# Scoring cached keys in sixteen small array tiles: keys turned by VectorE instead of TensorE

## The chip, the cores and the metric

The kernel runs on one core of one Trainium2 chip, in one launch. All arithmetic is in 32-bit floats. The metric is the device time in microseconds (us) from the first to the last instruction of the program; lower is better. Work on the core goes to TensorE (PE, matrix products out of SBUF into the eight PSUM banks), VectorE (DVE), ScalarE (ACT), GpSimd (POOL, here mostly an issuer of DMAs) and SyncE (SP, which only issues DMAs). Each engine runs its own instructions in order, and they meet through counting semaphores.

## What is computed

One decoder step: layer 0 has latent attention (MLA), layer 1 sliding-window attention, and each layer ends in a mixture of experts. Prompt tokens (512) and 8 sampled sequences of 4 new tokens go through it together. The change touches one thing alone, the attention of the sampled tokens over their cached past in layer 0:

```python
past = cache_pool[page_table].reshape(b, past_len, MLA_ROW)      # 8 x 4096 rows of 256 + 64
c_past, kr_past = past[..., :KV_LORA], past[..., KV_LORA:]
q_lat = jnp.einsum('bthd,chd->bthc', q_nope, w_uk)
s_past = (jnp.einsum('bthc,bkc->bhtk', q_lat, c_past).astype(jnp.float32)
          + jnp.einsum('bthr,bkr->bhtk', q_rope, kr_past).astype(jnp.float32)) * MLA_SCALE
...
p = jax.nn.softmax(jnp.concatenate([s_past, s_new], axis=-1), axis=-1).astype(c.dtype)
o_lat = (jnp.einsum('bhtk,bkc->bthc', p[..., :past_len], c_past)
         + jnp.einsum('bhtk,bkc->bthc', p[..., past_len:], c))
o = jnp.einsum('bthc,chd->bthd', o_lat, w_uv).reshape(b, t, MLA_HEADS * V_HEAD)
```

Each sequence has 32 query rows (8 heads, 4 tokens) and 4096 cached rows of 320 numbers, which lie in 32 pages of 128 rows, scattered in HBM and found through a page table.

## The kernel before

Everything is placed by hand: SBUF regions, PSUM banks, the order on each engine and every semaphore wait. The part around the change, which this text calls the cached stage, comes after the prompt's attention in layer 0 and before its output projection.

**Pages.** A page is loaded with its 128 rows on the 128 partitions, 320 floats each, 160 KB a page. Two SBUF buffers of 32 pages take turns (`pages[b % 2]`). Those of sequences 0 and 1 are loaded early by POOL. For b from 2 on, a buffer comes free in quarters of 8 pages as the value product of b - 2 passes over it: `page_mm` counts three of them, `pv_mm` the last. SP loads the first and third quarter, POOL the second and fourth. What this text calls quarter 1 of b is the first eight pages, semaphore `pages0` or `pages1`.

**Keys.** The value product wants cached rows on partitions, as they are loaded. The scores want the 320 features on partitions, so each page is transposed. For a quarter of a sequence (eight pages), `keys_T(b, t)` on PE makes 20 transposes of 128x128 (`flip`, L2021) into banks 2 to 6, ACT copies three banks and DVE two (L752, L1324) into `kT`, two buffers in turn, and `scores(b, t)` makes 12 products of 32 query columns by 256 keys over 128 or 64 features, in four column groups of the array (L2016), into banks 0 and 1.

**Softmax.** DVE takes the largest score of the first half, then of the second (`largest_so_far`, `largest`, L1329 and L1336), ACT makes the exponentials in two halves (`weigh`, L923 and L926), PE transposes the weights (`weights_T`), ACT and DVE copy them, and `values(b)` makes 33 products against the untransposed pages into bank 7.

**Order.** In PE's order one sequence is interleaved with the next: `keys_T(b, 0)`, `scores(b - 1, 3)`, `keys_T(b, 1)`, `scores(b, 0)`, `weights_T(b - 1)`, `values(b - 1)`, `keys_T(b, 2)`, `scores(b, 1)`, `keys_T(b, 3)`, `scores(b, 2)`.

**Ahead and behind.** Ahead of the loop the weight block `w_uk` is transposed (16 flips), the queries are multiplied by it (`qlat_mm`, 32 records), copied (L752, L1309, L1313), and the scores over the new tokens are made (`new_mm`). Behind the loop come the output projection, whose weights SP loads once `values(6)` is done (`mla_wo`), the router, and the experts, whose weights stream from HBM.

A 32-bit product appears in the trace as two pairs of LDWEIGHTS and MATMUL, a transpose as one; such a pair is called a record here. A line of a helper stands for all its callers: L2016 is every product, L2021 every transpose, L752 every copy by ACT.

Of the kernel before, what the change touches and what calls it, by code (L numbers as in the profile page):

```python
# [24 lines left out]
PAGES = 32  # L25
PHYS = 320
# [52 lines left out]
        tp_mm2 tp_mm3 tp_mm4 tp_mm5 tp_mm6""",  # L79
# [48 lines left out]


def keys_at(b, t):  # L130

    return 4 * b + t + max(0, b - (t < 2))


def weights_at(b):

    return 4 * (b + 1) + 2 + b if b < NB - 1 else 4 * NB + b
# [41 lines left out]
def build(nc, a, o):  # L179
    with ExitStack() as ctx:  # L180
# [118 lines left out]
        odd_pair = pair_buffers()  # L299
        qsw = m.take(TOK)  # L300
        even_pair = pair_buffers()
        qr, qn, kn, v_m = zip(even_pair, odd_pair)
        cqjunk = p_m[0][:, 0:QL]

        s = Arena(mem, pair_from - 2 * TOK, WORDS)
        kT_both = [s.take(5 * 4 * P) for _ in range(2)]
        kT = [q.rearrange("p (n g c) -> p n g c", n=5, g=2) for q in kT_both]
        wukT = kT_both[1][:, 0:H * 2 * P].rearrange("p (h k c) -> p h k c", h=H, k=2)
        p_s = s.take(8 * P)
        pT_s = cqT.rearrange("p k t -> p (k t)")[:, 0:8 * P].rearrange("p (n c) -> p n c", n=8)  # L310
        o_s = s.take(NB, CL)
        qlat = cqT.rearrange("p k t -> p (k t)")[:, 8 * P:8 * P + 2 * NB * NS].rearrange("p (k b q) -> p k b q", k=2, b=NB)
        qmix, qodd1, qodd2 = (s.take(NB, NS) for _ in range(3))
        sel32 = s.take(NS)
        over = Arena(mem, cq_at, cq_at + 2 * QL + CL + 2 * DR + QL)
        olatT = over.take(2, H, NS)
        smask = over.take(NB, NS)
# [3 lines left out]
        pTn = s.take(NS)  # L321
        mn, m_s, m2_s, nm_s, l_s, l2_s, ln_s, w_s = (s.take(NB) for _ in range(8))
        mg, lg_s, dg = (s.take(4, NB) for _ in range(3))
        mt, lt_s = (s.take(NB) for _ in range(2))
        assert s.at <= WORDS - 2 * 2 * H * DN and qsw.shape[1] == TOK
        wkvb = Arena(mem, WORDS - 2 * 2 * H * DN, WORDS).take(2, 2 * H * DN)
# [99 lines left out]
        def _(sp):  # L426
# [57 lines left out]
            for j in range(1, PAIRS):  # L484
                load_pair(j)
            sp.wait_ge(sig["qr_ready"], happened("qr_ready", PAIRS))
            sp.wait_ge(sig["o_mm"], happened("o_mm", UNITS - 2 * PT))
            sp.dma_start(wkvb, wkv).then_inc(sig["wkvb_in"], DMA)
# [115 lines left out]
        def _(g):  # L604
# [42 lines left out]
            def experts(L):  # L647
# [11 lines left out]
                g.wait_ge(sig["h_ready"], happened("h_ready", NORMED[2 * L + 1]))  # L659
                g.dma_start(gain, row(a["norm_ffn"][L])).then_inc(sig["gain_in"], DMA)  # L660
# [87 lines left out]
        def _(act):  # L748
# [160 lines left out]
            act.drain().then_inc(sig["wuk_act"], 1)  # L909

            def keys_T(b, t):

                at = keys_at(b, t)
                act.wait_ge(sig["qk_mm"], happened("qk_mm", 4 * b + t - 1))
                for bank, n in ((2, 0), (4, 1), (6, 2)):
# [1923 lines left out]
```

## Time and profile before

| | us |
|---|---|
| median of 3 runs | 1846.52 (1845.17 to 1849.54) |
| the profiled execution, its span | 1842.6 |
| TensorE busy | 1743.9 (95%) |
| VectorE busy | 602.8 (33%) |
| ScalarE busy | 381.9 (21%) |
| a period of the cached stage, from one value product's start to the next | 21.3 |

The page gives no time of the profiled execution apart from its span. The span is cut into 40 slices of 46 us; the cached stage fills slices 5 to 8. The granted clock of TensorE is given as a share of 2.4 GHz, so 0.50 is 1.2 GHz.

### The profile page before, as it was taken

What the parts mean: (1) busy time and instruction counts of PE and PEld (TensorE: products, weight loads), DVE (VectorE), ACT (ScalarE), POOL (GpSimd) and SP (SyncE); (2) the same over time, 40 slices, a digit from 0 to 9 for tenths busy, and PEclk for the clock granted to TensorE, in tenths of its full rate; (3) what the DMA queues carried; (4) which work ended last, traced back from release to release, by engine and by line L of the source; (5) the groups of instructions that cost most, each with busy time, mean ns of one, the idle gap of its engine ahead of it and who ended that gap; (6) DMA issues with size and microseconds to landing.
All of it is one profiled execution on the core that took longest, in us unless ns stands there. A gap on an engine that the chain in (4) does not pass through costs nothing.

```text
span 1842.6 us, 29042 instructions
## 1 busy us (share of the span) xinstructions
PE 1743.9 (95%) x9946; PEld 871.1 (47%) x9947; DVE 602.8 (33%) x1586; ACT 381.9 (21%) x858; POOL 214.1 (12%) x312
## 2 busy tenths in 40 slices
PE   7899899999899999999999899999899999999995
PEld 5466676655544444434344445455444444333342
DVE  2334343331522222222222556764322222212223
ACT  2233344431111111111011224342011111111112
POOL 1231014410001000000010201000000010000010
PEclk9899999999989999999999999999899999999998
DMA  6252137775449999999998800032899999999974
GB/s 181 68 155 88 50 116 237 254 253 208 159 182 404 414 421 417 412 419 419 415 418 350 303 14 1 20 138 85 347 375 412 422 414 418 414 421 408 418 307 151
DMA packets 80624, 511.63 MB, mean 278 GB/s; under 512 B 20917, under 2 KB 39302, under 8 KB 54074
## 3 DMA queue, kind: packets, MB, share of 16 engines
q1 hardware_dynamic: 61962, 461.35, 62.1%
q0 software_dynamic: 18576, 49.16, 8.1%
q8 instruction: 51, 0.84, 0.2%
q14 instruction: 35, 0.29, 0.1%
HBM read 498.07 MB, written 26.52 MB: 285 GB/s over the span
## 4 chain that ended last, share of the span: by engine, by line
PE 75%; DMA 14%; DVE 5%; issue 2%; ACT 2%; DVEq 1%; SPq 0%; POOL 0%; ACTq 0%; POOLq 0%
PE ps L2016 65%; DMA mem<-in_moe_w_up 11%; PE ps L2021 10%; ACT mem L752 1%; DMA mem<-in_x_sample 1%; DMA mem<-in_c_masks 1%; DVE mem L1794 0%; DMA mem<-moe_rows_back 0%; DMA mem<-in_cache_mla 0%; DMA moe_rows_back<-mem 0%; DVE mem L1765 0%; DMA mem<-in_swa_sinks 0%; DVE mem L1336 0%; ACT mem L923 0%; ACT mem L926 0%
## 5 line engine op out<-in xcount | busy, mean ns | idle before, releaser
L2016 PE MATMUL ps<-mem 128*64 128x512 f32 (+14 forms) x7970 | 1510.1, 485 | 62.2 <-DMA mem<-moe_rows_back 14.0
L2016 PEld LDWEIGHTS ps<-mem 128*64 128x64 f32 (+4 forms) x7970 | 641.9, 145 | 837.8 <-issue 747.6
L752 ACT ACTIVATE mem<-ps 128x512 f32<-128x512 f32 (+4 forms) x370 | 205.7, 567 | 621.9 <-PE ps L2016 425.2
L2021 PE MATMUL ps<-mem 128*128 128x128 f32 (+1 forms) x1976 | 274.8, 280 | 28.9 <-DMA mem<-in_x_prompt 6.9
L2021 PEld LDWEIGHTS ps<-mem 128*128 128x128 f32 (+1 forms) x1976 | 234.2, 171 | 125.0 <-issue 101.7
L1636 DVE TENSOR_TENSOR mem<-mem,ps 64x512 f32<-64x512 f32 x64 | 44.2, 690 | 433.2 <-ACT mem L995 433.2
L692 POOL DMA_INDIRECT moe_rows_back<-mem x64 | 57.3, 896 | 853.5 <-DVE mem L1653 842.6
L995 ACT ACTIVATE mem<-ps 64x512 f32<-64x512 f32 x64 | 37.7, 589 | 557.8 <-PE ps L2016 557.8
L1653 DVE COPY mem<-ps 64x512 f32<-64x512 f32 x64 | 44.4, 693 | 147.2 <-PE ps L2016 147.2
L1324 DVE COPY mem<-ps 128x512 f32<-128x512 f32 x64 | 44.2, 692 | 77.0 <-PE ps L2021 73.0
L644 POOL DMA_DIRECT2D mem<-in_cache_mla x96 | 51.7, 538 | 104.2 <-PE ps L2016 94.2
L1617 DVE COPY mem<-ps 64x512 f32<-64x512 f32 x32 | 22.2, 694 | 89.4 <-PE ps L2016 89.4
L624 POOL DMA_DIRECT2D mem<-in_cache_mla x64 | 34.4, 538 | 114.1 <-issue 114.1
L1062 ACT ACTIVATE mem<-mem 128x256 f32<-128x256 f32 (+1 forms) x64 | 30.3, 474 | 61.6 <-DVEq L1799 61.6
L682 POOL DMA_INDIRECT mem<-moe_rows_in,mem x34 | 33.2, 977 | 79.3 <-issue 79.3
L1794 DVE CUSTOM_DVE_ANT_0 mem<-ps,mem 128x256 f32<-128x256 f32 (+1 forms) x64 | 26.3, 448 | 27.2 <-PE ps L2016 25.1
L1561 DVE TENSOR_TENSOR mem<-mem 128x320 f32<-128x320 f32 x70 | 34.0, 486 | 2.1
L665 POOL DMA_DIRECT2D moe_rows_in<-mem x10 | 5.4, 538 | 237.8 <-DVE mem L1452 237.8
L1720 DVE SCALAR_TENSOR_TENSOR mem<-mem 128x1024 f32<-128x1024 f32 (+1 forms) x16 | 23.1, 1441 | 23.1 <-DMA mem<-moe_rows_back 21.8
L1644 DVE COPY mem<-ps 128x256 f32<-128x256 f32 x64 | 27.2, 425 | 8.1
L867 ACT ACTIVATE mem<-mem 128x128 f32<-128x128 f32 (+3 forms) x32 | 18.0, 561 | 37.8 <-DVEq L1273 37.8
L1622 DVE TENSOR_TENSOR mem<-ps,mem 128x512 f32<-128x512 f32 x32 | 22.1, 692 | 9.8 <-PE ps L2021 9.7
(237 smaller groups left out, 485.2 us busy)
## 6 DMA issues: line engine op xcount, KB each, us to landing
mem<-in_moe_w_gate SPq DMA_DIRECT2D x64, 2048.0 KB, 21.3
mem<-in_moe_w_up SPq DMA_DIRECT2D x64, 2048.0 KB, 27.8
mem<-in_moe_w_down SPq DMA_DIRECT2D x64, 2048.0 KB, 19.4
mem<-in_cache_mla POOLq DMA_DIRECT2D x160, 160.0 KB, 4.4
mem<-in_cache_mla SPq DMA_DIRECT2D x96, 160.0 KB, 5.5
mem<-moe_rows_back SPq DMA_DIRECT2D x8, 1024.0 KB, 8.7
mem<-in_mla_wo SPq DMA_DIRECT2D x1, 4096.0 KB, 14.1
moe_rows_in<-mem POOLq DMA_DIRECT2D x8, 512.0 KB, 3.0
```

The costliest lines, as they stand in the source:

```text
L624: g.dma_start(pages_flat[par][:, bass.ds(j * ROW, ROW)], a["cache_mla"][0][bass.ds(page, 1)].rearrange("a p c -> p (a c)")).then_inc(sig[f ...
L644: g.dma_start(pages[b % 2][:, j, :], a["cache_mla"][0][bass.ds(at[n], 1)].rearrange("a p c -> p (a c)")).then_inc(sig[f"late_pages{b % 2}" ...
L682: g.indirect_dma_start(out=xe[b][0:BLK, :], out_offset=None, in_=rows_in, in_offset=bass.IndirectOffsetOnAxis(ap=fetch_at[b][0:BLK, 0:1].b ...
L692: g.indirect_dma_start(out=rows_back, out_offset=bass.IndirectOffsetOnAxis(ap=store_at[b][0:BLK, 0:1].bitcast(U32), axis=0), in_=ye[b][0:B ...
L752: return act.activation(out, in_, ACT.Copy)
L995: act.activation(sg[BLK:2 * BLK, :], ps[0:BLK, b, :], ACT.Silu).then_inc(sig["silu_ready"], 1)
L1324: v.tensor_copy(kT[t % 2][:, n], ps[:, bank, :].rearrange("p (g c) -> p g c", g=2)).then_inc(sig[f"tp_ev{bank}"], 1)
L1561: v.tensor_tensor(onehot[b], rankm[:, :, cols(q, 1)].broadcast_to([P, TILES, BLK]), slots.unsqueeze(1).broadcast_to([P, TILES, BLK]), ALU. ...
L1636: v.tensor_tensor(hid[0:BLK, :], sg[BLK:2 * BLK, :], ps[BLK:2 * BLK, b, :], ALU.mult).then_inc(sig["hid_ready"], 1)
L1653: v.tensor_copy(ye[b][0:BLK, FF:D], ps[BLK:2 * BLK, 2 + b, :]).then_inc(sig["y1_ready"], 1)
L2016: return pe.matmul(out, lhsT, rhs, start=start, stop=stop)
L2021: return pe.transpose(out, in_, ident[at:at + n, at:at + n])
```

## The change

Pages are no longer transposed on TensorE. VectorE turns each quarter of a sequence, 128 partitions by 2560 floats, with one instruction that transposes 32x32 blocks in place of the 20 flips and five copies. In a block turned so, features lie on 32 partitions and 32 keys along the row, and the four groups of 32 partitions hold four groups of keys. So the query is copied to all four partition groups (`qrep`, made once by ten products with a selection matrix `pick`), and scores are made in sixteen 32x32 tiles of the array: tile (i, g) multiplies 32 features of one partition group i by 32 query columns into PSUM partitions 32g, for 128 keys, and ten such steps sum the 320 features. The scores of the four partition groups lie in banks 0 to 3. PE's order is now `weights_T(b - 1)`, `values(b - 1)`, `scores(b, 0)`, `scores(b, 1)`, and all softmax copies go to ACT. To make room the buffers are moved, `w_uk` and `w_uv` are loaded apart, and three loads get an added wait: `w_uv` for the last score, the MoE's first `down` weights for `oc_mm`, and POOL's load of `gain`, whose place now holds `p_s`.

```diff
+            def keys_T(b, n):
+
+                if b < 2 and n == 0:
+                    v.wait_ge(sig[f"late_pages{b % 2}"], landed(f"late_pages{b % 2}", PAGES))
+                if b >= 2:
+                    name, before_ = (("pages", 0), ("late_pages", PAGES), ("third_pages", 0), ("fourth_pages", 0))[n]
+                    v.wait_ge(sig[f"{name}{b % 2}"], landed(f"{name}{b % 2}", before_ + QUARTER * (b // 2)))
+                if n % 2 == 0:
+                    v.wait_ge(sig["qk_mm"], happened("qk_mm", max(2 * (b - 1) + n // 2 + 1, 0)))
+                v.transpose(keysT[n // 2][:, n % 2 * QUARTER * ROW:(n % 2 + 1) * QUARTER * ROW],
+                            pages_flat[b % 2][:, n * QUARTER * ROW:(n + 1) * QUARTER * ROW]).then_inc(sig["keysT_ready"], 1)
+
+            def largest(b):
+
+                v.wait_ge(sig["qk_mm"], happened("qk_mm", 2 * b + 2))
+                v.tensor_reduce(m_s[:, b:b + 1], ps[:, 0:4, 0:2 * P], XY, ALU.max)
+                v.drain()
+                v.tensor_scalar(nm_s[:, b:b + 1], m_s[:, b:b + 1], mn[:, b:b + 1], -MLA_SCALE, ALU.max, ALU.mult
+                                ).then_inc(sig["nms_ready"], 1)
...
-            for b in range(NB):
-                if b:
-                    keys_T(b, 0)
-                    largest(b - 1)
-                keys_T(b, 1)
-                if b:
-                    weights_T(b - 1)
-                keys_T(b, 2)
-                keys_T(b, 3)
-                largest_so_far(b)
+            for b in range(1, NB):
+                keys_T(b, 0)
+                largest(b - 1)
+                for n in range(1, 4):
+                    keys_T(b, n)
             largest(NB - 1)
...
+            for j in range(ROW // 32):
+                rows, q = (slice(0, P), qlat[:, j // 4]) if j < 8 else (slice(0, DR), qmix[0:DR])
+                last = mm(ps[:, j // 2, j % 2 * NB * NS:(j % 2 + 1) * NB * NS], pick[rows, j % 4, :], q.rearrange("p b q -> p (b q)"), True, True)
+                if j % 2:
+                    last.then_inc(sig["qrep_mm"], 1)
+
+            def scores(b, half_):
+
+                if half_ == 0:
+                    pe.wait_ge(sig["p_s_ready"], happened("p_s_ready", 2 * b))
+                pe.wait_ge(sig["keysT_ready"], happened("keysT_ready", 4 * b + 2 * half_ + 2))
+                blocks = keysT[half_].rearrange("p (m g c) -> p m g c", m=4, g=4)
+                c0 = half_ * P
+                for j in range(ROW // 32):
+                    for i in range(4):
+                        rows = slice(32 * i, 32 * (i + 1))
+                        for g in range(4):
+                            last = mm(ps[g * NS:(g + 1) * NS, i, c0:c0 + P].rearrange("p (m k) -> p m k", m=4),
+                                      qrep[rows, j, b, :], blocks[rows, :, g, 32 * j:32 * (j + 1)], j == 0, j == ROW // 32 - 1)
                 last.then_inc(sig["qk_mm"], 1)
...
             for b in range(NB):
-                keys_T(b, 0)
-                if b:
-                    scores(b - 1, 3)
-                keys_T(b, 1)
-                scores(b, 0)
                 if b:
                     weights_T(b - 1)
                     values(b - 1)
-                keys_T(b, 2)
+                scores(b, 0)
                 scores(b, 1)
-                keys_T(b, 3)
-                scores(b, 2)
-            scores(NB - 1, 3)
             weights_T(NB - 1)
             values(NB - 1)
```

VectorE before, from the score maximum of one sequence through the next one's (L1324 copies turned keys out of PSUM, L1336 is the maximum, L1345 and L1347 copy turned weights):

```order
L1336 TENSOR_REDUCE mem<-ps 128x1 [waits qk_mm]
L1338 TENSOR_SCALAR mem<-mem 128x1
L1324 COPY mem<-ps 128x512 [waits tp_mm3,qk_mm]
L1324 COPY mem<-ps 128x512 [waits tp_mm5]
L1345 COPY mem<-ps 128x512 [waits pv_mm,tp_mm3]
L1347 COPY mem<-ps 32x32 [waits tp_mm6]
L1324 COPY mem<-ps 128x512 [waits tp_mm3,qk_mm]
L1324 COPY mem<-ps 128x512 [waits tp_mm5]
L1324 COPY mem<-ps 128x512 [waits tp_mm3,qk_mm]
L1324 COPY mem<-ps 128x512 [waits tp_mm5]
L1329 TENSOR_REDUCE mem<-ps 128x1 [waits qk_mm]
```

VectorE in the changed kernel, the same place, from `keys_T(2, 0)` on (L1315 turns a quarter, L1321 is the maximum of sequence 1):

```order
L1315 STREAM_TRANSPOSE mem<-mem 128x2560 [waits qk_mm,pages0]
L1321 TENSOR_REDUCE mem<-ps 128x1 [waits qk_mm]
L1323 TENSOR_SCALAR mem<-mem 128x1
L1315 STREAM_TRANSPOSE mem<-mem 128x2560 [waits late_pages0]
L1315 STREAM_TRANSPOSE mem<-mem 128x2560 [waits qk_mm,w_a_in]
L1315 STREAM_TRANSPOSE mem<-mem 128x2560 [waits consts_in]
L1315 STREAM_TRANSPOSE mem<-mem 128x2560 [waits qk_mm,pages1]
L1321 TENSOR_REDUCE mem<-ps 128x1 [waits qk_mm]
```

The waits for arriving pages (`pages0` and `pages1` are quarter 1; `w_a_in` and `consts_in` are the semaphores that quarters 3 and 4 of an even sequence share) were PE's and are VectorE's now, and the first of them stands ahead of the maximum of the sequence before.

TensorE in the changed kernel, one sequence (L2007 is the product helper, L2012 the transpose helper):

```order
L2012 MATMUL ps<-mem 128x128 [waits pT_s_ready,p_s_ready]
L2012 MATMUL ps<-mem 128x128 x3
L2012 MATMUL ps<-mem 128x128 [waits pT_s_ready,p_s_ready]
L2012 MATMUL ps<-mem 128x128 x3
L2012 MATMUL ps<-mem 32x32 [waits pTn_ready]
L2007 MATMUL ps<-mem 32x256 [waits pT_s_ready,o_s_ready]
L2007 MATMUL ps<-mem 32x256 x15
L2007 MATMUL ps<-mem 32x256 [waits pT_s_ready]
L2007 MATMUL ps<-mem 32x256 x15
L2007 MATMUL ps<-mem 32x256 [waits pTn_ready]
L2007 MATMUL ps<-mem 32x128 [waits keysT_ready,p_s_ready]
L2007 MATMUL ps<-mem 32x128 x159
```

Nothing of the next sequence stands between a sequence's last score and its weights any more, and the scores are 320 products a sequence where there were 48.

## Rows read from the trace of the kernel before

**Rows 1.** The page: busy time by engine, and the chain that ended last.

```profile
PE 1743.9 (95%) x9946; PEld 871.1 (47%) x9947; DVE 602.8 (33%) x1586; ACT 381.9 (21%) x858; POOL 214.1 (12%) x312
PE 75%; DMA 14%; DVE 5%; issue 2%; ACT 2%; DVEq 1%; SPq 0%; POOL 0%; ACTq 0%; POOLq 0%
```

**Rows 2.** Busy time per engine in one period, with clock and DMA.

```profile
core 0: us, PE busy (x) PEld busy (x) DVE busy (x) ACT busy (x) POOL busy (x), PEclk, DMA share, GB/s
275.08:296.40 21.32, 21.00 (x251) 14.42 (x252) 7.97 (x15) 9.69 (x20) 8.61 (x16) 1.00 0.75 248
```

**Rows 3.** Timeline of a period: start, length, engine, line, operation, idle before.

```profile
253.79 4.21 PE L2016 MATMUL ps<-mem 128*32 128x256 f32 x66 [0.28 <-ACT mem L752]
...
261.83 2.40 PE L2021 MATMUL ps<-mem 128*128 128x128 f32 x20
...
264.16 1.64 PE L2016 MATMUL ps<-mem 128*32 128x256 f32 x24
```

**Rows 4.** Weight loads of PE near the first pages' arrival.

```profile
265.73 2.17 PEld L2021 LDWEIGHTS ps<-mem 128*128 128x128 f32 x20 [0.41 <-DMA mem<-in_cache_mla]
```

**Rows 5.** DMA between 253.8 and 275.1, in 40 slices.

```profile
DMA  0010554929999979999999999999999999411000
GB/s 0 0 31 0 120 183 77 327 75 351 387 366 406 224 262 356 373 366 325 358 365 380 392 385 361 351 368 375 368 358 346 339 368 313 167 55 46 5 0 0
```

**Rows 6.** The tail of the cached stage, timeline.

```profile
395.76 0.69 DVE L1336 TENSOR_REDUCE mem<-ps 128x1 f32<-128x512 f32 x1 [2.09 <-PE ps L2016]
396.78 0.69 ACT L923 ACTIVATE mem<-ps,mem 128x512 f32<-128x512 f32 x1 [3.59 <-DVE mem L1338]
397.64 0.66 PE L2021 MATMUL ps<-mem 128*128 128x128 f32 x4 [1.94 <-ACTq L925]
398.81 0.79 PE L2021 MATMUL ps<-mem 128*128 128x128 f32 x5 [0.52 <-ACTq L930]
398.84 0.23 ACT L955 ACTIVATE mem<-mem 32x32 f32<-32x32 f32 x1
399.96 6.48 PE L2016 MATMUL ps<-mem 128*32 128x256 f32 x67 [0.36 <-ACT mem L752]
405.85 0.38 ACT L752 ACTIVATE mem<-ps 128x256 f32<-128x256 f32 x1 [6.03 <-PE ps L2016]
```

**Rows 7.** Granted clock of PE in four stretches.

```profile
222.40:232.70 10.30, 8.04 (x37) 0.50 0.01 2
399.90:403.30 3.40, 3.34 (x32) 0.51 0.00 0
403.40:405.70 2.30, 2.30 (x38) 1.00 0.04 7
1198.66:1199.57 0.91, 0.91 (x60) 1.00 0.79 270
```

**Rows 8.** VectorE's groups by form: total, mean ns.

```profile
L1324 DVE COPY mem<-ps 128x512 f32<-128x512 f32 x64 | 44.2, 692 | 77.0 <-PE ps L2021 73.0
L1720 DVE SCALAR_TENSOR_TENSOR mem<-mem 128x1024 f32<-128x1024 f32 x12 | 15.4, 1285 | 22.3 <-DMA mem<-moe_rows_back 21.8
L1561 DVE TENSOR_TENSOR mem<-mem 128x320 f32<-128x320 f32 x70 | 34.0, 486 | 2.1
L1281 DVE TENSOR_SCALAR mem<-mem 128x512 f32<-128x512 f32 x8 | 3.9, 486 | 0.7
```

**Rows 9.** The stretch ahead of the loop, timeline.

```profile
212.00 0.49 DVE L1281 TENSOR_SCALAR mem<-mem 128x512 f32<-128x512 f32 x1
217.44 0.69 DVE L1305 COPY mem<-ps 128x512 f32<-128x512 f32 x1 [4.95 <-PE ps L2021]
219.15 4.01 PE L2016 MATMUL ps<-mem 128*128 128x32 f32 x32 [0.88 <-DVE mem L1305]
225.42 3.18 PE L2016 MATMUL ps<-mem 128*128 128x32 f32 x12 [2.26 <-DVEq L1315]
232.96 1.57 DVE L1354 TENSOR_TENSOR mem<-ps,mem 32x32 f32<-32x32 f32 x8
```

**Rows 10.** The 128 small products of layer 1's samples, timeline of PE.

```profile
1195.42 4.33 PE L2016 MATMUL ps<-mem 64*128 64x256 f32 x130
```

**Rows 11.** The page: the load of the output weights, us to landing.

```profile
mem<-in_mla_wo SPq DMA_DIRECT2D x1, 4096.0 KB, 14.1
```

More of the change, by code:

```diff
@@ L11 @@
 X = mybir.AxisListType.X
+XY = mybir.AxisListType.XY
 P = 128
@@ L284, in build, with pair_buffers @@
         ptab = m.take(NB * PAGES, dt=I32)
+        samples_from = m.at
+        def pair_buffers():
+            return m.take(SEQ), [m.take(SEQ) for _ in range(2)], [m.take(SEQ) for _ in range(2)], m.take(PT, 2 * DN)
+        qsw = m.take(TOK)
+        even_pair = pair_buffers()
         cosT = m.take(TOK)
         sinT = m.take(TOK)
-        pair_from = m.at
         wqp = m.take(3, 2 * (DN + DR))
@@ L320, in build @@
         pn = over.take(NB, NS)
[L321 to L326, printed above, removed]
         r = Arena(mem, work, moe_end)
@@ L493, in _ @@
             sp.dma_start(wo_m, a["mla_wo"][0].rearrange("(k p) n -> p k n", p=P)).then_inc(sig["wo_in"], DMA)
+            sp.wait_ge(sig["qk_mm"], happened("qk_mm", 2 * NB))
+            for k in range(2):
+                sp.dma_start(wuv[:, k], wkv_heads[:, k, :, 1, :]).then_inc(sig["wkvb_in"], DMA)
             def experts(L):
@@ L905, in _ @@
             act.wait_ge(sig["qlat_mm"], happened("qlat_mm", 1))
-            for dst, at in ((qlat[:, 1], slice(0, P)), (qodd1[DR:P], slice(0, DR)), (qodd2[0:DR], slice(DR, P))):
-                copy(dst.rearrange("p b (h t) -> p b h t", h=H),
-                     ps[at, 5, 0:H * NS].rearrange("p (h b t) -> p b h t", h=H, b=NB))
+            copy(qlat[:, 1].rearrange("p b (h t) -> p b h t", h=H),
+                 ps[:, 5, 0:H * NS].rearrange("p (h b t) -> p b h t", h=H, b=NB))
             act.drain().then_inc(sig["wuk_act"], 1)
[L911 to L915, printed above, removed]
-                    count = 4 * b + t if bank == 4 else at
-                    act.wait_ge(sig[f"tp_mm{bank}"], happened(f"tp_mm{bank}", count + 1))
-                    copy(kT[t % 2][:, n], ps[:, bank, :].rearrange("p (g c) -> p g c", g=2)).then_inc(sig[f"tp_ev{bank}"], 1)
+            for n in range(0, 5, 2):
+                act.wait_ge(sig["qrep_mm"], happened("qrep_mm", n + 1))
+                copy(qrep[:, 2 * n:2 * n + 2], ps[:, n, :].rearrange("p (j b q) -> p j b q", j=2, b=NB)
+                     ).then_inc(sig["qrep_act"], 1)
@@ L941, in values @@
                 copy(o_s[:, b, :], ps[:, 7, 0:CL]).then_inc(sig["o_s_ready"], 1)
-            for b in range(NB):
-                keys_T(b, 0)
-                if b:
-                    weigh(b - 1)
-                keys_T(b, 1)
-                if b:
-                    weights_T(b - 1)
-                    values(b - 1)
-                keys_T(b, 2)
-                keys_T(b, 3)
+            for b in range(NB - 1):
+                weigh(b)
+                weights_T(b)
+                values(b)
             weigh(NB - 1)
@@ L1350, in _ @@
+            v.drain().then_inc(sig["qlat_ready"], 1)
+            keys_T(0, 2)
+            for n in range(1, 5, 2):
+                v.wait_ge(sig["qrep_mm"], happened("qrep_mm", n + 1))
+                v.tensor_copy(qrep[:, 2 * n:2 * n + 2], ps[:, n, :].rearrange("p (j b q) -> p j b q", j=2, b=NB)
+                              ).then_inc(sig["qrep_dve"], 1)
+            keys_T(0, 3)
             v.wait_ge(sig["new_mm"], happened("new_mm", 1))
@@ L1409, in add_out @@
                 if n == NS:
-                    out[1] = kT_both[0][0:n, 0:FF]
+                    out[1] = keysT[0][0:n, 0:FF]
                     v.tensor_copy(out[1], ps[n:2 * n, 2 + 2 * (n_ % 2) + 1, :])
```

194 lines of the change are left out of this document (72 added, 122 removed).

## The prediction

> **What bounds the kernel now.** I read the page's busy times and its chain first, then one period of the cached stage as a window by engine, then its timeline, weight loads and DMA, and last the stretches before and behind it. TensorE is busy 95% of the span and 75% of the chain [rows 1]. In one period of the cached stage, 21.32 us, it works 21.00 us at full clock, while VectorE works 7.97, ScalarE 9.69, and the DMA engines 0.75 of the time [rows 2]. So PE sets this stage, and what is taken from it counts until something else ends last. The timeline tells what can be taken: 20 transposes hold PE 2.33 us from start to start, and the 24 records of a quarter's scores 1.57 us [rows 3]. A period has four of each. I call A the start of a value product (253.79 for sequence 0).
>
> **What goes from PE.** 4 x 2.33 = 9.3 us of transposes and 4 x 1.57 = 6.3 us of scores, 15.6 of the 21.3 us. 5.7 us stay: the value product and the transposes of weights.
>
> **What comes to PE.** 320 products, 640 records of 128 keys a sequence. The old scores ran six rounds of four tiles, 256 keys wide, in 1.57 us [rows 3]: a round of 4 records took 0.26 us and 256 keys alone need 0.11 at 2.4 GHz for each, so the four lay side by side. If all sixteen tiles do so too, a half of a sequence is 20 rounds of 16 records with 128 keys, each half a round of 256 keys, 0.13 us: 2.6 us. The 0.26 has the fill of the array and the hand-over in it once per six rounds, here it is once per twenty, so I take 2.3, and 4.6 a sequence. The bounds: if each of the 640 records costs what the densest stretch of the profile shows, 0.91 / 60 = 15 ns [rows 7], it is 9.7 us; by the 128 small products of layer 1 (4.33 us for 130 records with the wait, about 29 ns each [rows 10]) it is 18.4; and if the four row groups take turns, 4 x 4.6 = 18.4 again. PE has room for much of that: the period below leaves it 8 us idle.
>
> **What comes to VectorE.** A turn of 128 x 2560 floats, four a sequence. No row shows the operation. Two reads and a write of 1024 floats take 1285 ns and of 320 take 486 ns, 1.135 ns a float and 123 ns fixed, so 2560 floats take 3.0 us; the 512 floats of a TENSOR_SCALAR in 486 ns are 0.71 ns each, so 1.9 us; the copy out of PSUM, 692 ns for 512, gives 3.46 us [rows 8]. I take 2.8, nearer the upper row, as a turn leaves no float out; the range is 1.9 to 3.5, and 5.6 if it has to go over the data twice. With 2.8, VectorE works 11.2 + 1.5 us a period for turns and the maximum of 1024 scores, less than the period; it would set the period only from (21.3 - 1.5) / 4 = 4.9 us a turn. What VectorE loses, eight copies, and what ScalarE loses, twelve, was hidden behind PE.
>
> The Trainium skill, "Vector Engine (DVE) Microarchitecture Reference", section 3.8, has the transpose sustain one element per cycle in each lane; no row here shows it. By it a turn would be an estimated 2.7 to 2.8 us, and the sum would not move.
>
> **The new wait.** On VectorE `keys_T(b+2, 0)` stands ahead of the maximum of b+1, and waits for quarter 1 of b+2, which the value product of b frees. Behind it on VectorE stand that maximum and all further turns, and for the maximum wait the weights, and so PE's next value product. Before, quarter 1 of sequence 2 let PE go at 265.73 [rows 4], A + 11.9. DMA is nearly idle up to about A + 1.5, then at about 360 GB/s to about A + 18 [rows 5]; the four quarters are freed within 4.2 us and share that rate, hence the late first one. The period is now a chain:
> - A to the arrival of quarter 1: 11.9;
> - the turn: 2.8;
> - from the maximum to the next value product: the tail of the stage shows it without other work on PE. Start of the maximum to start of the exponentials 396.78 - 395.76 = 1.02, plus 0.53 as the maximum now reads 1024 floats, not 512 (at some 1 ns a float); from the exponentials to the value product 399.96 - 396.78 = 3.18, less 0.23 for a small copy whose place changes: 4.5 [rows 6].
>
> Sum 19.2. PE idles some 8 us of it. What idling does to its clock the tail shows: after idling 1.94, 0.52 and 0.36 us PE ran 32 records at clock 0.51 for 3.4 us (1.2 GHz), then at 1.00, so that the value product took about 5.8 and not 4.2 us [rows 6, 7]. A slow start frees the first quarter up to 1.1 us later. So a period lies between 19.2 and 20.3; I take 19.8, and 19.3 for the first one, whose value product follows work. With arrivals 1 us earlier or later, and the bounds of the turn, it is 18.4 to 21. PE's own work is off the path: the value product 5.8, scores 4.6, done at A + 10.4, before the turn is (A + 14.7). DMA's load is off it too: 5.24 MB a period at 360 GB/s is 14.6 us.
>
> **The head.** VectorE's last unit operation ahead is at 212.0 to 212.5 [rows 9]. Two turns of sequence 0 then take 5.6 us to 218.1, while the copy of the transposed `w_uk` stood at 217.44; so the latent queries start at 219.8 and end, with 4.0 us, at 223.9, 0.7 later. The new wait for `qrep` follows: 20 records of 128 x 256. At half clock, which this stretch had before (0.50 [rows 7]), they take 20 x 0.43 = 8.5 us by twice the streaming of a full one, at full clock 4.3; I take 6.4, since part of it waits for copies. From about 224.5 that is 230.9. The new tokens' products (3.18 us for 12 [rows 9]) take 2.2 as part of their wait falls away, to 233.1; the scores of sequence 0 end at 237.8, PE having waited for nothing else, and its maximum follows `keys_T(1, 0)` at 238.4, which is a turn of pages long there. Plus 4.5: A(0) = 243.0 against 253.79, a gain of 10.8 us. The bounds of qrep give 2 us either way.
>
> **The sum.** A(6) = 243.0 + 19.3 + 5 x 19.8 = 361.3. No page is waited for at the end, so A(6) to A(7) is the value product 5.8, scores at about 5.3 (partly at the lower clock), 4.5 and a small copy of 0.3: 15.9. A(7) = 377.2 against 399.96 [rows 6]: 22.8 us less. Of it the head gives 10.8, six periods, 118.3 for 127.8, give 9.5, and the last one, 15.9 for 18.4, gives 2.5.
>
> What lies behind moves along if nothing is late there. The output weights are loaded once `values(6)` is done, 361.3 + 5.8 = 367.1, and take 14.1 us [rows 11]: 381.2, two us before `values(7)` ends at 383. Thin cover; without it up to 1 us. `w_uv`'s 1 MB lies behind the prompt's output projection, the waits of `down` and `gain` behind loads whose users come tens of us later: nothing; were the cover gone, 1 to 3 us. So the profiled execution, 1842.6, becomes 1819.8. The median of the runs shown is 3.9 above that execution: 1823.7, forecast 1824. Its own range, with periods of 18.4 to 21 (6 x 1.3 either way), the head's 2 and the small products' 15 ns bound (not on the path, +5 in the last period), is 1812 to 1834.
>
> **Rivals.**
> 1. *Small products don't fit side by side (slower).* One mechanism: each of the 640 records of a sequence starts too late after the one before, or row groups take turns, 18.4 us a sequence. Then PE's chain is values 5.8, scores 18.4, maximum to values 4.5, small copy 0.2: a period of 28.9, against 21.3. With A(0) 14 later, at 256.8, and seven periods A(7) is 459, 59 us later: about 1905. It decides from (21.3 - 5.8 - 4.7) / 640 = 17 ns a record. For it: layer 1's 29 ns [rows 10]. Against it: 15 ns over 60 records [rows 7], and the four column tiles that ran together [rows 3]. Chance 0.10.
> 2. *A floor on starts.* As one mechanism here: each pair of records starts no closer to the next pair than layer 1's small ones, 29 ns less their wait, some 25 ns a record: 16 us a sequence, a period of 5.8 + 16 + 4.7 = 26.5, 5.2 more than before seven times and 3 or 4 for the head: about 40 us slower, 1887. 60 records in 0.91 us [rows 7] and 24 in 1.57 speak against it only in part, as a product's two halves may start together. Chance 0.05. The Trainium skill, "TensorE: Matmul & The Clock Gate", section "Wait — 56ns, not 53.3ns?", states such a floor, "Start-to-start never drops below ≈25 ns however small N is"; by it the kernel would be slower, and the row with 15 ns disagrees. The same page, in its part on array tiling, reports sixteen 32-row, 32-column tiles as 10.6 times as quick, with 512 columns each; here they have 128, which no row shows.
> 3. *VectorE becomes the bound.* A turn goes over its data twice, 5.6 us. Four of them and 1.5 for the maximum are 23.9 us a period, 2.6 more than before, six times 15.6; the head's two turns take 5.6 longer and the first one after them 2.8, 8.4 of its gain of 10.8, and the last period is as forecast: 15.6 - 2.4 - 2.5 = 10.7 slower. Chained to the arrival of quarter 1 (11.9 + 5.6 + 4.5 = 22.0) it is less than that, so VectorE's own sum holds, but every quarter that VectorE then turns late frees its buffer and the maximum late by up to another 1.5 us a period: 11 to 20, about 1862. For it: nothing shown; against it: all forms of rows 8 within 1.9 to 3.5. Chance 0.09.
> 4. *The gain is given back.* Quarter 1 arrives 1.5 us later still with the slow clock, and `qrep` waits: a period of 21.3 and no gain ahead: 1846 or a little less. Chance 0.08.
> 5. *Quicker.* Value products at the lower clock free the quarters over 5.8 us, so quarter 1 has DMA more to itself and lands at A + 10: a period of 17.5, 12 us less: about 1810. Chance 0.08.
>
> The forecast has 0.60. Below 0.2% (3.7 us) a difference can't be told from none in this kernel. Faster: 0.60, 0.08 of rival 5, 0.02 of rival 4: 0.70. Same: 0.06. Slower: 0.10 + 0.05 + 0.09 = 0.24. The range of 1808 to 1872 leaves out rivals 1 and 2, and little below it.
>
> **What would show it.** Right: L1315 about 2.8 us each, and before every first one of a sequence an idle stretch ended by the page DMA at A + 12; the maximum directly behind it; 320 records of scores in 2.3 us; PE idle 8 us a period, with clock 0.5 at the start of the value product; periods of 19.8; A(0) near 243. Wrong: scores of 320 records over 5 us a half (rivals 1, 2); L1315 over 4.9 us with VectorE without gaps (3); an arrival past A + 13 (4) or before A + 10.5 (5); PE waiting for the output weights behind `values(7)`.

## The result and the profile after

The changed kernel takes 1925.11 us (median of 4 runs, 1921.22 to 1928.52) where the kernel before takes 1845.85: a ratio of 1.0436 (95% interval 1.0412 to 1.0461), 79 us slower. The forecast was 1824, its range 1808 to 1872.

In the page of the changed kernel, busy times, the chain and the queue that brings instructions answer to [rows 1]:

```profile
PE 1742.9 (90%) x13678; PEld 869.4 (45%) x13679; DVE 638.5 (33%) x1522; ACT 333.2 (17%) x779; POOL 214.1 (11%) x312
q8 instruction: 80, 1.31, 0.3%
PE 72%; DMA 14%; issue 5%; DVE 5%; ACT 1%; DVEq 1%; SPq 0%; ACTq 0%; POOLq 0%
L1315 DVE STREAM_TRANSPOSE mem<-mem 128x2560 f32<-128x2560 f32 x32 | 89.2, 2822 | 73.5 <-PE ps L2007 73.3
```

TensorE is busy as long as before, in 84 us more. A turn takes 2.8 us, as forecast. What has grown is "issue", from 2% of the chain to 5%: time in which an engine waited for nothing that the profile shows as a wait. The line `q8 instruction` says 80 packets in 1.31 MB, 16 KB a packet; the page before has 51:

```profile
q8 instruction: 51, 0.84, 0.2%
```

The value products now start at 254.18, 287.56, 319.27, 351.82, 385.27, 416.78, 450.13 and 482.89. The first is where it was (253.79); the last is 82.9 us later (399.96). Nearly all of the 84 us, 82.5, is lost in these seven periods of 32.7 us on average. One period as a window, against [rows 2]:

```profile
core 0: us, PE busy (x) PEld busy (x) DVE busy (x) ACT busy (x) POOL busy (x), PEclk, DMA share, GB/s
254.18:287.56 33.38, 20.12 (x716) 13.87 (x716) 12.49 (x7) 3.50 (x11) 8.58 (x16) 0.65 0.49 160
```

PE idles 13 us in it at a mean clock of 0.65. Its timeline, against [rows 3] (start, length, ..., in brackets the idle time before and what ended it):

```profile
254.18 7.51 PE L2007 MATMUL ps<-mem 128*32 128x256 f32 x242
265.94 2.59 PE L2007 MATMUL ps<-mem 32*32 32x128 f32 x128 [4.25 <-issue]
272.69 2.84 PE L2007 MATMUL ps<-mem 32*32 32x128 f32 x128 [4.16 <-issue]
276.69 2.82 PE L2007 MATMUL ps<-mem 32*32 32x128 f32 x128 [1.16 <-issue]
280.69 2.04 PE L2007 MATMUL ps<-mem 32*32 32x128 f32 x80 [1.19 <-issue]
285.17 2.46 PE L2012 MATMUL ps<-mem 128*128 128x128 f32 x9 [2.44 <-ACTq L930]
```

Small products run in bursts of exactly 128 records, 256 instructions of PE. Between bursts PE stands still, 1.2 us when DMA is quiet and 4.2 while pages load. VectorE is no cause; it has turned quarter 1 at 276.4 and then waits for PE:

```profile
273.54 2.85 DVE L1315 STREAM_TRANSPOSE mem<-mem 128x2560 f32<-128x2560 f32 x1 [14.43 <-PE ps L2007]
282.77 1.23 DVE L1321 TENSOR_REDUCE mem<-ps 128x1 f32<-128x1024 f32 x1 [6.38 <-PE ps L2007]
```

Two periods of the changed kernel (287.56 to 351.82) and two of the kernel before (275.08 to 317.7), packets of the instruction queue with MB and share:

```profile
q8 instruction: 11, 0.18, 1.1%
```

```profile
q8 instruction: 4, 0.07, 0.7%
```

So PE's instructions come in packets of 16 KB, one for 256 instructions or 128 records: 11 against 4 in two periods. Over the span PE has 13,679 - 9,947 = 3,732 records more, 29.2 times 128, and 80 - 51 = 29 packets more.

The trace has every packet of this queue by itself, and the pauses end with them. In the period shown packets start at 263.27, 270.11, 274.35 and 278.10 and take 1.05, 1.12, 0.93 and 1.09 us; the bursts start at 265.94, 272.69, 276.69 and 280.69, each 1.4 to 1.6 us after its packet has landed. All 33 pauses of over 0.6 us that stand before or between small products in this stage end so, 1.2 to 1.6 us behind a packet. Beside page loads a packet takes no longer than without; it starts later, 4.2 us after the burst at 265.94 and 1.7 and 1.4 us after the next two. Where DMA is quiet a packet shows by itself, as one slice of 66 GB/s in the view of DMA from 272 to 282, 40 slices of 0.25 us (at 278.0 and at 281.75):

```profile
GB/s 359 348 348 261 197 128 67 67 46 112 51 31 0 0 0 0 0 0 0 0 0 0 0 0 66 0 0 0 0 0 0 0 0 0 0 0 0 0 0 66
```

Behind its wait for the softmax PE runs about two packets' worth without a pause: the seven periods start with 216 to 318 records (here 242) before the first one. The score products of the eight sequences, by form:

```profile
L2007 PE MATMUL ps<-mem 32*32 32x128 f32 x5120 | 103.4, 363 | 72.8 <-issue 72.8
```

Per sequence that is 12.9 us in bursts and 9.1 us standing, 22.0 us, where the forecast had 4.6. With it a period is 5.8 + 22.0 + 4.7 = 32.5, where 32.7 was measured.

The Trainium skill describes this supply in "Runtime: NRT & Kernel Launch", section "Instruction fetch mechanics": instruction memory is refilled in blocks of 16 KiB, 256 instructions, and crossing a block costs little, "mostly hidden". The packets here have that size. In the kernel before they are hidden; in the changed one they are not.

### The profile page after: what moved, and what is told of

Its sections match the earlier page's. It is cut to its first block, busy times and chain, and to the rows that moved or that the text cites. A ratio compares the mean times of both kernels' runs of the same rounds, so it can differ in the third digit from the quotient of the medians.

```text
span 1926.9 us, 36219 instructions
## 1 busy us (share of the span) xinstructions
PE 1742.9 (90%) x13678; PEld 869.4 (45%) x13679; DVE 638.5 (33%) x1522; ACT 333.2 (17%) x779; POOL 214.1 (11%) x312
## 3 DMA queue, kind: packets, MB, share of 16 engines
q8 instruction: 80, 1.31, 0.3%
## 4 chain that ended last, share of the span: by engine, by line
PE 72%; DMA 14%; issue 5%; DVE 5%; ACT 1%; DVEq 1%; SPq 0%; ACTq 0%; POOLq 0%
PE ps L2007 66%; DMA mem<-in_moe_w_up 12%; PE ps L2012 7%; DMA mem<-moe_rows_back 1%; ACT mem L926 1%; DVE mem L1321 1%; DVE mem L1711 0%; DVE mem L1785 0%; DMA mem<-in_mla_w_a 0%; DMA moe_rows_back<-mem 0%; DVE mem L1756 0%; DMA mem<-in_mla_wq_b 0%; DVE mem L1748 0%; DVE mem L1749 0%; ACT mem L758 0%
## 5 line engine op out<-in xcount | busy, mean ns | idle before, releaser
L2007 PE MATMUL ps<-mem 32*32 32x128 f32 (+12 forms) x12342 | 1575.2, 445 | 131.0 <-issue 79.2
L2007 PEld LDWEIGHTS ps<-mem 32*32 32x32 f32 (+5 forms) x12342 | 706.7, 140 | 915.8 <-issue 834.6
L758 ACT ACTIVATE mem<-ps 128x512 f32<-128x512 f32 (+5 forms) x291 | 157.0, 548 | 590.1 <-PE ps L2007 436.5
L2012 PE MATMUL ps<-mem 64*128 64x64 f32 (+4 forms) x1336 | 205.3, 288 | 45.5 <-ACTq L930 19.8
L2012 PEld LDWEIGHTS ps<-mem 64*128 64x128 f32 (+4 forms) x1336 | 167.7, 188 | 133.0 <-issue 89.7
L1315 DVE STREAM_TRANSPOSE mem<-mem 128x2560 f32<-128x2560 f32 x32 | 89.2, 2822 | 73.5 <-PE ps L2007 73.3
L628 POOL DMA_DIRECT2D mem<-in_cache_mla x64 | 34.5, 538 | 114.6 <-issue 114.6
L926 ACT ACTIVATE mem<-ps,mem 128x512 f32<-128x512 f32 x16 | 11.0, 687 | 183.9 <-DVE mem L1323 183.1
L1321 DVE TENSOR_REDUCE mem<-ps 128x1 f32<-128x1024 f32 x8 | 9.8, 1225 | 81.3 <-PE ps L2007 81.3
L1635 DVE COPY mem<-ps 128x256 f32<-128x256 f32 x64 | 27.2, 425 | 8.1
L1711 DVE SCALAR_TENSOR_TENSOR mem<-mem 128x1024 f32<-128x1024 f32 (+1 forms) x16 | 22.4, 1402 | 21.4 <-DMA mem<-moe_rows_back 20.6
```

What stands on the lines that cost most here:

```text
L628: g.dma_start(pages_flat[par][:, bass.ds(j * ROW, ROW)], a["cache_mla"][0][bass.ds(page, 1)].rearrange("a p c -> p (a c)")).then_inc(sig[f ...
L758: return act.activation(out, in_, ACT.Copy)
L1315: v.transpose(keysT[n // 2][:, n % 2 * QUARTER * ROW:(n % 2 + 1) * QUARTER * ROW], pages_flat[b % 2][:, n * QUARTER * ROW:(n + 1) * QUARTE ...
L2007: return pe.matmul(out, lhsT, rhs, start=start, stop=stop)
L2012: return pe.transpose(out, in_, ident[at:at + n, at:at + n])
```

## The experiments

The theory: such a packet, from here on a block, of 256 PE instructions takes about 3.5 to 3.8 us to come, longer beside other DMA traffic, and 5.6 blocks a period set the pace. Rivals: (A) the sixteen tiles take turns in the array, so streaming counts; (B) a floor between starts; (C) the forecast's chain over VectorE's wait for pages; (D) VectorE's turning disturbs PE. All are single runs beside a single run of the kernel before on the same chip, save the changed kernel and the two by feature, which are medians of 4, 4 and 12 runs; runs of one of these kernels lie up to 17 us apart, so a few us between single runs say nothing. "First" is where value product 0 starts, "period" the mean of the six periods behind it, "last" the seventh, in which no pages are loaded but the 4 MB of output weights are.

| kernel | time | before | first | period | last | packets of q8 |
|---|---|---|---|---|---|---|
| before (profile of the prediction) | 1846.52 | | 253.79 | 21.4 | 17.8 | 51 |
| changed | 1925.11 | 1845.85 | 254.2 | 32.7 | 32.8 | 80 |
| 32 keys a product | 1920.67 | 1842.98 | 254.8 | 31.2 | 31.8 | 80 |
| small page loads | 1890.56 | 1842.98 | 252.9 | 27.2 | 32.3 | 80 |
| both | 1886.78 | 1840.41 | 255.5 | 26.0 | 31.4 | 80 |
| 256 keys, behind four turns | 1864.98 | 1842.98 | 246.4 | 25.2 | 26.0 | 60 |
| maximum first | 1928.74 | 1842.98 | 254.3 | 32.9 | 32.8 | 80 |
| before, split eightfold | 1989.08 | 1850.71 | 273.2 | 39.8 | 32.7 | 93 |
| half the products | 1831.77 | 1850.71 | 243.3 | 20.6 | 21.0 | 60 |
| a fifth of the products | 1822.41 | 1850.71 | 243.3 | 20.4 | 12.9 | 48 |
| a fifth, maximum first | 1819.08 | 1850.71 | 239.9 | 18.4 | 19.4 | 48 |
| before, small page loads | 1841.13 | 1840.41 | 254.2 | 21.3 | 17.8 | 51 |
| buffers by feature | 1887.22 | 1844.49 | 250.3 | 29.1 | 19.5 | 60 |
| by feature, maximum first | 1841.40 | 1844.98 | 245.2 | 22.6 | 20.1 | 60 |

**Streaming cut to a quarter.**

```diff
-  mm(ps[g * NS:(g + 1) * NS, i, c0:c0 + P]..., qrep[rows, j, b, :], blocks[rows, :, g, 32 * j:32 * (j + 1)], ...)
+  mm(ps[g * NS:(g + 1) * NS, i, c0:c0 + 32], qrep[rows, j, b, :], blocks[rows, 0, g, 32 * j:32 * (j + 1)], ...)
```

> The changed kernel with each of its 320 score products per sequence cut from 128 keys to 32 (three quarters of the keys are not scored; the weights made from them are stale). Same number of records, a quarter of the streaming. Theory (TensorE's instructions come in blocks of 256, that is 128 records, and a block takes 3.5 to 3.8 us to come, 6.5 to 7 while pages load): periods stay at 32.7, time 1925 within 8. Rival A (the sixteen tiles stream one after another): the records' time falls to a quarter, periods near 20, about 1830. Rival B (a floor of some 25 ns between starts): time as in the theory, but no gaps between bursts of 128 records.

1920.67 us. The timeline of PE in its fourth period:

```profile
359.14 1.53 PE L2007 MATMUL ps<-mem 32*32 32x32 f32 x128 [4.12 <-issue]
365.61 1.53 PE L2007 MATMUL ps<-mem 32*32 32x32 f32 x128 [4.94 <-issue]
369.34 1.53 PE L2007 MATMUL ps<-mem 32*32 32x32 f32 x128 [2.20 <-issue]
373.34 0.81 PE L2007 MATMUL ps<-mem 32*32 32x32 f32 x55 [2.48 <-issue]
```

The bursts shrink to 1.53 us and the pauses grow: starts stay 6.5 us apart beside the loads and 3.7 to 4.0 without, as in the changed kernel. The period falls by 1.5 us only. Rival A falls. So does B as it was put, for 1.53 us for 128 records is 12 ns each, here at half clock (the row's columns are those of the window above: PE busy 1.53, weight loads 1.40, PEclk 0.50):

```profile
359.14:360.67 1.53, 1.53 (x128) 1.40 (x128) 0.00 (x0) 0.00 (x0) 1.39 (x3) 0.50 1.09 395
```

**Page loads of one row.**

```diff
-  sp.dma_start(pages[b % 2][:, j, :], a["cache_mla"][0][bass.ds(at[n], 1)]...)
+  sp.dma_start(pages[b % 2][0:1, j, :], a["cache_mla"][0][bass.ds(at[n], 1), 0:1]...)   # and the same for POOL
```

> The changed kernel with each page load from sequence 2 on moving one row of 128 (the other rows keep old data), same number of DMAs and waits. Theory: what makes a block of instructions late is first its own 3.7 us, and on top the pages' traffic; without the traffic the gap between bursts is 0.9 to 1.6 us everywhere, 5.6 blocks a period at 3.7 give 21 to 23 us, time about 1855. Rivals A and B (the array itself or a floor between starts): periods stay above 30, time 1915 or more.

1890.56 us, 34.5 less than the changed kernel; periods of 27.2, where I had expected 21 to 23 and a time of about 1855. A period again has 5.6 blocks at 3.5 to 4.0 us, 20.7, but hardly any comes while PE waits 4.7 us for the softmax (none starts between 328.17 and 335.36), and that I had not added; with it the sum is 25.4. PE from 315.93:

```profile
315.93 1.90 PE L2007 MATMUL ps<-mem 32*32 32x128 f32 x128 [1.06 <-issue]
319.66 2.59 PE L2007 MATMUL ps<-mem 32*32 32x128 f32 x128 [1.83 <-issue]
323.12 2.81 PE L2007 MATMUL ps<-mem 32*32 32x128 f32 x128 [0.87 <-issue]
327.12 2.63 PE L2007 MATMUL ps<-mem 32*32 32x128 f32 x106 [1.19 <-issue]
```

Starts are 3.73, 3.46 and 4.00 us apart, whether the burst takes 1.90 or 2.81. The last period, with the load of the output weights in it, is 32.3 as in the changed kernel: the load of weights delays the blocks as that of pages does. Windows of two bursts show what the clock does to them:

```profile
315.93:317.80 1.87, 1.87 (x128) 1.53 (x128) 0.00 (x0) 0.00 (x0) 1.46 (x3) 1.00 0.08 13
297.84:300.60 2.76, 2.76 (x128) 2.13 (x128) 0.00 (x0) 0.00 (x0) 0.00 (x0) 0.50 0.03 6
```

15 ns a record at full clock, 22 at half. The Trainium skill, "TensorE: Matmul & The Clock Gate", section "Wait — 56ns, not 53.3ns?", has a floor of about 25 ns between starts; these runs disagree, with 15 ns for 128 keys and 12 ns for 32.

**Both edits, and the control.**

> The changed kernel with both edits, 32 keys a product and one row a page load. Theory (blocks set the pace, about 3.7 us from one burst of 128 records to the next without traffic, whatever the array does in them): as with small loads alone, bursts 3.4 to 4.0 us apart, bursts themselves 1.5 us, periods of 25 to 27.5, time 1880 to 1891. If in the run with small loads the array's own time set the pace: periods of 20 or less, 1845.

> A control: the kernel before, with each page load from sequence 2 on moving one row of 128. It has 251 records a period, two blocks of instructions in 21.3 us, so their coming is hidden even beside the traffic. Theory: periods of 21.3, time within 3 us of before. If the 35 us that the same edit took from the changed kernel came from less traffic as such (memory reads of TensorE or VectorE): 10 to 35 us faster here too.

1886.78 us with periods of 26.0, and PE with next to no array work and no traffic still starts a block every 3.5 to 3.7 us:

```profile
315.81 1.42 PE L2007 MATMUL ps<-mem 32*32 32x32 f32 x128 [2.15 <-issue]
319.54 1.56 PE L2007 MATMUL ps<-mem 32*32 32x32 f32 x128 [2.31 <-issue]
323.27 1.54 PE L2007 MATMUL ps<-mem 32*32 32x32 f32 x128 [2.17 <-issue]
326.73 1.36 PE L2007 MATMUL ps<-mem 32*32 32x32 f32 x106 [1.92 <-issue]
```

The kernel before loses nothing and gains nothing by small loads (1841.13 beside 1840.41): two blocks in 21.3 us are hidden.

**Twice the keys in a product.** Both halves in one product, `p (h m g c)`, 320 records a sequence, behind all four turns.

> The changed kernel with both halves of a sequence in one product of 256 keys: 160 products, 320 records a sequence, the same streaming in the same sixteen tiles; the maximum stands ahead of all four turns. Theory: 3.1 blocks a period, and the scores begin only behind four turns: a period of 22 to 25, time 1850 to 1875. Rival A (streaming): no fewer columns, and less overlap with the turns: 1925 to 1950. Rival B (floor of 25 ns): 8 us a period less, less what the turns give back, 1890.

1864.98 us, with periods of 25.2, just over the 22 to 25 that I had expected: 60 us off with the same number of columns streamed, and 20 packets less (80 to 60; 2,560 records less are 20.0 times 128).

**The maximum first on VectorE.**

```diff
-  keys_T(b, 0)
   largest(b - 1)
-  for n in range(1, 4):
+  for n in range(4):
       keys_T(b, n)
```

> The changed kernel with one edit on VectorE: the maximum of the sequence before stands ahead of the first turn of a sequence instead of behind it. Theory: the wait that my forecast was built on is not on the path, since the scores end 6 us after that turn: 1925 within 4, perhaps 1 slower where the turn now follows the maximum. Rival C (the forecast's chain over the arrival of quarter 1 still costs something): 5 to 20 us faster.

1928.74 us, 3.6 over the median and about at the top of the changed kernel's own runs (1928.52). Rival C falls for this kernel.

**The kernel before with its products split.** Each product of 256 keys becomes eight of 32, on the tiles that it had.

> The kernel before with each score product of 256 keys split into eight of 32: 768 score records a sequence instead of 96, the same streaming, the same four tiles, no turning on VectorE. Theory (the count of TensorE instructions alone): 923 records a period are 7.2 blocks, 2.2 of them during the loads and 5 at 3.6 us: a period of 30 to 33, time 1910 to 1935. Rival A (32-row tiles are what is slow) and rival D (VectorE's turning disturbs TensorE's reads): no more than 20 us over before, 1865 at most.

1989.08 us, periods of 39.8: slower still than the theory's 30 to 33 and 1910 to 1935, so the count of blocks alone does not explain this kernel. Packets rise from 51 to 93, by 42; 8 x 672 records more are 42.0 times 128. PE in two places of its second period:

```profile
287.35 1.00 PE L2016 MATMUL ps<-mem 128*32 128x32 f32 x29
289.01 3.63 PE L2016 MATMUL ps<-mem 128*32 128x32 f32 x127 [0.66 <-issue]
293.99 1.11 PE L2016 MATMUL ps<-mem 64*32 64x32 f32 x36 [1.35 <-issue]
...
299.03 5.38 PE L2016 MATMUL ps<-mem 128*32 128x32 f32 x192
```

Here most of the time is no pause: 192 records take 5.38 us, 28 ns each at clock 1.00, and at that pace a block lasts 3.6 us, so its successor is just in time. The window of the second place, without its last 0.1 us:

```profile
299.03:304.30 5.27, 5.27 (x193) 5.22 (x192) 0.11 (x1) 0.60 (x1) 0.00 (x0) 1.00 0.01 3
```

The weight loads fill 5.22 of these 5.27 us. Instructions are dear in a kernel without small row tiles and without turning on VectorE, which speaks against D as the cause; but the split shows a second price, that of starting a record, beside the supply. It is twice that of the 32-row tiles at full clock (28 against 15 ns). The full weight loads suggest that they set it; no run here tests that. The few pauses that are left end as in the changed kernel, those at 289.01 and 293.99 1.4 us after a packet has landed.

**Fewer products.** The feature loop runs over 5 or 2 blocks of ten.

> The changed kernel with five of the ten feature blocks left out of the scores: 320 records a sequence of 128 keys. Theory: 3.1 blocks a period, as many as with 256 keys a product, and here not behind four turns: a period of 21 to 23, time 1840 to 1860.

> The changed kernel with eight of the ten feature blocks left out of the scores: 128 records a sequence. Theory: 1.6 blocks a period, so instructions are no bound any more, and what remains is the chain of the forecast (arrival of quarter 1 at A + 11.9, turn 2.8, maximum to value product 4.5): a period of 19 to 20.5, time 1820 to 1835. If the chain was wrong too: a period of 12 to 17, time under 1810.

> The same with 128 score records a sequence, and the maximum ahead of the first turn on VectorE. If the forecast's chain is what bounds the run without this edit, the period falls from 19 to 20.5 to what DMA allows, 15 to 16.5, and the time by 20 to 30 us. If not, nothing changes.

1831.77, 1822.41 and 1819.08 us. Half of the products came out a little better than expected, periods of 20.6 for 21 to 23 and 1831.77 for 1840 to 1860. It has 2,560 records and 20 packets less than the changed kernel, a fifth of the products 4,096 records and 32 packets less, 20.0 and 32.0 times 128.

With a fifth of the products the first value product starts at 243.26 (forecast 243.0), six periods take 20.4 on average (19.8), and the last value product starts at 378.8 (377.2). Part of the match at the end is luck: the six periods lie between 19.0 and 23.5 and are 4.3 us longer in sum, and the last one is 3.0 shorter (12.9, forecast 15.9). The chain of the forecast stands in VectorE's rows there, the turn waiting for pages and the maximum right behind it:

```profile
290.24 1.53 PE L2007 MATMUL ps<-mem 32*32 32x128 f32 x64 [2.54 <-DVE mem L1315]
295.68 2.85 DVE L1315 STREAM_TRANSPOSE mem<-mem 128x2560 f32<-128x2560 f32 x1 [5.50 <-DMA mem<-in_cache_mla]
298.45 1.19 DVE L1321 TENSOR_REDUCE mem<-ps 128x1 f32<-128x1024 f32 x1
```

The turn starts 13.5 us after that value product (282.14), where I had 11.9. Moving the maximum ahead gave 2.0 us a period and 3.3 in all, not the 15 to 16.5 a period and the 20 to 30 in all that I had expected. The last value product starts 8.9 us earlier (369.9), but what lies behind it took 5.5 us longer in that single run. After a first one of 13.6 the periods stop at 18.8 to 20.2. What ends last is SP and POOL. In the period from 311.42, and in the next, each issues its sixteen page loads in this time:

```profile
318.90 9.47 SPq L458 DMA_DIRECT2D mem<-in_cache_mla  x16
...
321.07 9.69 POOL L648 DMA_DIRECT2D mem<-in_cache_mla  x16 [9.12 <-issue]
...
337.71 10.38 SPq L458 DMA_DIRECT2D mem<-in_cache_mla  x16
```

Between 328.4 and 337.7 SP reads the next sixteen page numbers, some 0.55 us each. 9.5 + 9.3 = 18.8 us is the distance between the two rows of SP. That this bounds the period follows from these rows; no run took it away.

**A complete kernel with 320 records.** Buffers hold half of the features of all pages, so a product spans 256 keys and halves still overlap.

```diff
-  v.transpose(keysT[n // 2][:, n % 2 * QUARTER * ROW:...], pages_flat[b % 2][:, n * QUARTER * ROW:...])
+  v.transpose(keysT[n // 2][:, n % 2 * QUARTER * ROW:...].rearrange("p (n c) -> p n c", n=HALF),
+              pages[b % 2][:, n % 2 * HALF:(n % 2 + 1) * HALF, n // 2 * (ROW // 2):(n // 2 + 1) * (ROW // 2)])
...
-  for j in range(ROW // 32):
+  for j in range(5 * half_, 5 * half_ + 5):
```

> A complete kernel from the changed one: the two key buffers hold half of the features of all 32 pages instead of all features of half of the pages, so a score product spans 256 keys (160 products, 320 records a sequence) and the second half can still be turned beside the first half's products. Theory (blocks of instructions): 395 records a period are 3.1 blocks, as in the run with half of the products left out (periods of 18.7 to 23), and TensorE's chain at half clock is 5.8 + 320 x 32 ns (10.2) + 4.7 = 20.7: periods of 19.5 to 22, value product 0 at 244 to 247, time 1825 to 1848. Rival A (streaming of the tiles is what counts): as long as the changed kernel, 1900 or more.

> The kernel with key buffers split by feature, and now the maximum ahead of all turns of the next sequence on VectorE. In the run without this edit the maximum stood behind two turns that wait for all four quarters of the sequence after next (the last lands 20 us after the value product's start), which gave periods of 28 to 29.7: the same chain that the forecast of the change rested on, 20 + 2.8 + 4.6 there. Without it TensorE's own chain is left: value product 5.8, 320 records in 10 to 12 us with the wait for one block of instructions, 4.7 to the next value product: periods of 20.5 to 23.5, value product 0 at 245 to 248, time 1832 to 1858. If the chain was not the cause: 1887 as without the edit.

The first took 1887.22 us, ratio 1.0217 (1.0183 to 1.0251), where I had expected 1825 to 1848: the maximum stood behind turns that now wait for all four quarters, and the forecast's chain became the bound, in a period from 339.01:

```profile
353.06 2.85 DVE L1316 STREAM_TRANSPOSE mem<-mem 128x2560 f32<-128x2560 f32 x1 [11.84 <-DMA mem<-in_cache_mla]
359.45 2.85 DVE L1316 STREAM_TRANSPOSE mem<-mem 128x2560 f32<-128x2560 f32 x1 [3.55 <-DMA mem<-in_cache_mla]
362.22 1.18 DVE L1322 TENSOR_REDUCE mem<-ps 128x1 f32<-128x1024 f32 x1
```

With the maximum first it takes 1841.40 us, 46 less; ratio to the kernel before 0.9987 (0.9967 to 1.0007), no difference that can be told. Its periods of 22.6 still hold pauses for blocks:

```profile
332.80 9.22 PE L2007 MATMUL ps<-mem 128*32 128x256 f32 x254
345.13 4.05 PE L2007 MATMUL ps<-mem 32*32 32x256 f32 x128 [3.11 <-issue]
351.87 0.62 PE L2007 MATMUL ps<-mem 32*32 32x256 f32 x4 [2.69 <-issue]
```

## Why the prediction was wrong

The sign and the time were wrong through one term of the sum: scores at 4.6 us a sequence. They take 22.0, because the coming of PE's instructions, which the sum put at nothing, sets their pace.

- *Scores, 4.6 us.* I took a round of sixteen records to cost half of a round of four with twice the keys. That is array time. The time of a record is no array time here: a burst has 15 ns a record at full clock and 22 at half, 12.9 us a sequence over all, and the blocks' waits add 9.1. Nor do the two simply add: with bursts of 1.5 us the waits grew and the period fell by 1.5 us only. My bound of 9.7 us (15 ns from [rows 7]) was right for a burst at full clock; I kept it out of the sum because PE had 8 us of idle time to take it up. Even the 12.9 us alone would make a period of 5.8 + 12.9 + 4.7 = 23.4, over the old 21.3 (a sum; no run shows it by itself). One reading was off as well: 4.33 us for 130 records [rows 10] are 33 ns each and not 29, so that bound was 21.3 us and not 18.4.
- *What the trace before could tell.* PE's instructions were counted nowhere in my working. 640 records are five blocks of instructions, and the page before gives 51 packets with 0.84 MB; I read that line and did not ask what sets their pace. It shows no pause for them in the cached stage, so their 3.7 us could not be read from it. What could be read is how far I went beyond it: the densest products of that stage, 66 records in 4.21 us [rows 3], use up a block in 8.2 us, and my 2.3 us for 320 records meant one in 0.9.
- *Rival 1* named the place, the direction and the chain (values, scores, maximum to values) and a price of 28.9 us a period; measured is 32.7. Its point of decision, 17 ns a record, was passed: 22.0 us are 34 ns. Its time of 1905 is 20 short. Its mechanism was half of it, slow starts; that row groups take turns is refuted. The other half, supply, was in no rival. It had 0.10, and rival 2 with 1887 had 0.05.
- *VectorE's turn, 2.8 us:* right (2.82). Rival 3 falls.
- *The new wait, period 19.8:* right as a mechanism and never reached in this kernel. In the run with a fifth of the products it sets 20.4, with quarter 1 at A + 13.5 in the period shown, past the A + 13 that was to be rival 4's sign, and in the first kernel by feature 29.1. Removing it there gave 46 us, here nothing.
- *The head, value product 0 at 243.0:* 254.2 in the changed kernel, as the scores of sequence 0 also come in bursts; 243.26 with few products.
- *PE's clock:* I gave idle PE half clock at the start of a value product only. In the period shown it is 0.65 on average, and the bursts run mostly at 0.50.
- *Behind the loop:* of 82.9 us at the last value product the span shows 84.3, 1.4 more. From the last value product on, the fourteen profiled runs take 1439.6 to 1447.5 us, so these 1.4 us need no cause.

## What to carry to other kernels

Count instructions as a resource of their own where one product becomes many: in this kernel TensorE used about two blocks of 256 (128 records in 32-bit each) without a pause behind an idle stretch, and further ones came no faster than one in about 3.5 to 3.7 us, and one in about 6.5 beside page loads at some 360 GB/s. A tile scheme that fills the array is worth only what is left after records x start time and blocks x fetch time, so make each product wide before it is made small in the array: the three kernels with 256 keys a product in place of 128 were 38 to 84 us quicker than the changed one. And where a kernel idles on "issue" between equal bursts, compare the packets of the instruction queue in the page with those of the kernel before.

## What the runs showed of the hardware

- Bursts of exactly 128 records and one 16 KB packet for each: 29 more packets for 3,732 more records, 42 for 5,376, 20 fewer for 2,560, 32 fewer for 4,096. In the changed kernel the bursts start 1.2 to 1.6 us after a packet has landed; a packet takes 0.9 to 1.4 us, with and without page loads beside it.
- Small tiles in all sixteen positions started 12 ns apart with 32 keys at half clock, and with 128 keys 15 ns apart at full and 22 at half clock. Products on 128 rows and 32 columns with 32 keys started 28 ns apart at full clock, with weight loads busy for 5.22 of 5.27 us.
- A turn of 128 x 2560 floats by VectorE takes 2.8 us, 1.1 ns a float in each partition, with contiguous input and with input in pieces of 160 floats alike (2.82 and 2.83).
- A queue that reads sixteen page numbers and issues sixteen loads of 160 KB needed 18.8 us for them; the 32 loads that two such queues share are 14.6 us at 360 GB/s.
